# Two-block network on one core: the attentions with heads of 64 weigh standing values with scaled, turned weights, two heads beside each other

## The reference, cut to what matters

```python
p = softmax(concat([sink, s_loc, s_ctx]))[..., 1:]          # 8 heads
o = einsum(p[:span], v_near) + einsum(p[span:], v_ctx)      # 64 wide
o_x = concat([o, local_mixers(...)]) @ w_out
x = layer_norm(ALPHA * x + g1 * o_x, ln1_g, ln1_b)
```

```python
ya = sliding_window_attention(qa, ka, va, sinks) * silu(g_a)   # 2 key heads
yb = forgetting_attention(qb, kb, vb, log_f) * silu(g_b)       # 8 key heads
yc = rms_norm(ssd_chunked(...) * silu(z_c), ssm_norm_w)
x = x + concat([ya, yb, yc]) @ w_out
```

## Time and profile before

| | |
|---|---|
| median of 3 runs | 2305.1 us |
| the profiled execution | 2304.22 us, span 2302.4 us |
| TensorE busy | 2035.6 us, 88% of the span |
| VectorE, ScalarE, GpSimd busy | 786.6 us, 457.2 us, 189.7 us |
| mean granted TensorE clock | 0.985 |
| the chain that ended last | PE 62%, DMA 31%, DVE 4%, ACT 2% |
| weighing in attentions (L541) | 512 records, 65.5 us busy |
| turns (L507) | 332 records, 61.1 us busy |

### The profile page before, as it was taken

One profiled execution on the slowest core, in us unless ns is written; L12 is line 12 of the kernel. 1 busy time (PEld: TensorE's weight loads), 2 busy tenths in 40 slices (PEclk: granted clock), 3 DMA queues, 4 the chain that ended last, 5 costly groups with the idle time before them and its releaser, 6 DMA issues.

```text
span 2302.4 us, 30476 instructions
## 1 busy us (share of the span) xinstructions
PE 2035.6 (88%) x11971; PEld 1212.3 (53%) x11972; DVE 786.6 (34%) x1836; ACT 457.2 (20%) x1059; POOL 189.7 (8%) x240
## 2 busy tenths in 40 slices
PE   6999999799877789999877777798999999999998
PEld 4566566444433335757433333344875575775574
DVE  1355674111111116656111111114466312456413
ACT  2142112111111112411111111111123212123112
POOL 1000001111111110001111111111000000000000
PEclk9999999999999999999999999999999999999999
DMA  9235649999999985686999999996343332343230
GB/s 376 110 129 240 255 156 378 423 426 427 427 425 426 425 345 211 236 317 257 424 425 425 424 425 425 427 420 242 134 182 129 111 147 110 147 165 129 95 142 19
DMA packets 62872, 640.95 MB, mean 278 GB/s; under 512 B 15868, under 2 KB 16420, under 8 KB 24240
## 3 DMA queue, kind: packets, MB, share of 16 engines
q1 hardware_dynamic: 41728, 588.39, 61.9%
q0 software_dynamic: 19984, 44.74, 5.5%
q10 hardware_dynamic: 1056, 6.37, 0.7%
HBM read 622.50 MB, written 44.17 MB: 290 GB/s over the span
## 4 chain that ended last, share of the span: by engine, by line
PE 62%; DMA 31%; DVE 4%; ACT 2%; issue 1%; SPq 0%; POOL 0%; DVEq 0%
DMA ring<-in_moe 26%; PE ps L866 10%; PE ps L1037 10%; PE ps L519 8%; PE ps L1051 6%; PE ps L1148 5%; PE ps L507 3%; PE ps L695 3%; DMA ring<-in_denseA 3%; PE ps L1220 2%; PE ps L872 2%; PE ps L1016 2%; PE ps L541 2%; PE ps L771 2%; PE ps L584 1%; DMA ring<-in_denseB 1%
## 5 line engine op out<-in xcount | busy, mean ns | idle before, releaser
L866 PE MATMUL ps<-ring,scr 128*64 128x256 f32 (+1 forms) x4800 | 667.5, 430 | 178.2 <-DMA ring<-in_moe 169.3
L866 PEld LDWEIGHTS ps<-ring,scr 128*64 128x64 f32 x4800 | 333.4, 138 | 485.9 <-DMA ring<-in_moe 239.3
L1833 DVE TENSOR_TENSOR scr<-ps,scr 128x512 f32<-128x512 f32 (+3 forms) x98 | 54.6, 558 | 574.6 <-PE ps L866 487.0
L1037 PE MATMUL ps<-ring,hT 128*128 128x512 f32 (+1 forms) x576 | 245.5, 578 | 5.1 <-ACT hT L1546 5.1
L519 PE MATMUL ps<-ring,hT 128*128 128x512 f32 (+1 forms) x512 | 199.3, 547 | 0.5 <-ACT hT L1516 0.5
L1444 POOL DMA_INDIRECT ys_scratch<-scr,ytab x128 | 125.0, 976 | 825.4 <-DVE scr L2495 791.6
L1670 ACT ACTIVATE scr<-ps 128x512 f32<-128x512 f32 x64 | 38.2, 597 | 760.8 <-PE ps L866 694.0
L2495 DVE COPY scr<-ps 128x1024 f32<-128x1024 f32 x64 | 78.4, 1224 | 269.3 <-PE ps L866 243.4
L1037 PEld LDWEIGHTS ps<-ring,hT 128*128 128x128 f32 x576 | 108.1, 193 | 117.8 <-issue 108.2
L1516 ACT ACTIVATE scr<-ps 128x256 f32<-128x256 f32 (+2 forms) x168 | 71.3, 436 | 403.7 <-PE ps L507 403.7
L519 PEld LDWEIGHTS ps<-ring,hT 128*128 128x128 f32 x512 | 97.3, 193 | 93.0 <-issue 89.2
(11 more groups left out here) (330 smaller groups left out, 2019.2 us busy)
## 6 DMA issues: line engine op xcount, KB each, us to landing
ring<-in_moe SPq DMA_DIRECT2D x192, 2048.0 KB, 15.9
ring<-in_denseB SPq DMA_DIRECT2D x48, 2048.0 KB, 7.7
ring<-in_denseA SPq DMA_DIRECT2D x36, 2048.0 KB, 16.2
scr<-ys_scratch POOLq DMA_DIRECT2D x6, 1024.0 KB, 7.2
modB<-mod_scratch POOLq DMA_DIRECT2D x10, 512.0 KB, 11.3
ring<-kv_scratch SPq DMA_DIRECT2D x2, 2048.0 KB, 8.6
tok_scratch<-hb POOLq DMA_DIRECT2D x6, 512.0 KB, 2.9
memT_scratch<-modB ACTq DMA_DIRECT2D x2, 1024.0 KB, 6.7
```

The costliest lines, as they stand in the source:

```text
L866: last = mm(out, lhs(c)[:, 0:64], w(c)[:, half * q:half * (q + 1)], start=(c == 0), stop=(c == n - 1))
L1037: last = mm(T["open"][:, 0:cols], hT16[:, c, t * P:(t + 1) * P], w[:, c, 0:cols], start=(c == 0), stop=(c == DC - 1))
L1833: return V.tensor_tensor(out, a, b, op)
```

## The change

The function `attention` becomes two: `memory_attention` for the heads of 256, which keeps the old scheme, and `paired_attention` for the heads of 64. In this one

- VectorE takes the scores of two units, then waits for each unit's exponential, takes the reciprocal of its sum, and multiplies `sbuf_p` by it in place; a new semaphore `p_scaled` tells TensorE that it can turn. Then come the extras of two units. Pieces of the extras move by a unit or two;
- the sink's score is one more column in `sbuf_s`, so that the exponential's sum holds it; the question and answer about `esk` go;
- the values stand and the turned weights pass, 128 columns: the outputs come by columns, 64 by 128 queries for a head. An even head uses partitions 0 to 63 of the bank, an odd head 64 to 127; the products of two heads alternate by key block. A bank holds the 8 heads of 128 queries, and VectorE copies it;
- ScalarE takes both exponentials, then copies both turned units, then serves the questions of two units;
- the turns of the attentions' outputs go, in A (16 blocks in layer 0, 8 in layer 1) and in B (16 in each layer), with ScalarE's copies of them; the products with the output weights read `hb` and `mixB`. The norm's scratch rows move from `hb` to the place of `sbuf_pT`;
- the gates `ga` and `gb` of B come by columns, as the attentions' outputs now do.

The old functions are in the section above; the diff's core:

```diff
-TURNED = ("x0", "x1", "x2", "qb", "kb")
+TURNED = ("x0", "x1", "x2", "qb", "kb", "ga", "gb")
...
-    sbuf_s = cv(2, 512)
-    sbuf_p = cv(2, 512)
+    sbuf_s = cv(2, 516)
+    sbuf_p = cv(2, 516)
...
+        def turn_weights(i, nkc):
+            turn([sbuf_p[:, i % 2, k * P:(k + 1) * P] for k in range(nkc)])
+        def paired_attention(units, score, values, nkc, fill):
+            T["p"] += len(units)
+            for i in range(2):
                 score(*units[i])
+            fill(0)
+            for i in range(0, len(units), 2):
+                n, h = units[i]
+                for k in (i, i + 1):
+                    need("scaled", p_scaled)
+                    turn_weights(k, nkc(n))
+                    turned = T["tp"]
+                    if k == i:
+                        for at in range(i + 2, min(i + 4, len(units))):
+                            score(*units[at])
+                    if k > 0:
+                        fill(k)
+                if h == 0:
+                    T["bank"] = av_bank()
+                pe.wait_ge(tp_free, turned)
+                for b in range(nkc(n)):
+                    for q in range(2):
+                        last = mm(T["bank"][HD * q:HD * q + HD, h // 2 * P:(h // 2 + 1) * P], values(n, h + q, b),
+                                  sbuf_pT[:, q, b, :], start=(b == 0), stop=(b == nkc(n) - 1))
+                if h == NH - 2:
+                    last.then_inc(av_full, 1)
...
+        def memory_attention(units, score, values, beside):
...
-            for t in range(nt):
-                need("h", h_ready)
-                turn([hb[:, t, i * P:(i + 1) * P] for i in range(4)])
+            need("h", h_ready, nt)
...
-                    of_rows(mk_at - 2 + j, t, 0, 512)
+                    w = tile(mk_at - 2 + j)
+                    rows_times(lambda c: hb[:, t, c * P:(c + 1) * P] if c < 4 else hT8[:, c, t * P:(t + 1) * P],
+                               lambda c: w[:, c, :], 512)
...
-                if i == 12:
+                if i == 13:
                     pe.wait_ge(sums_ready, l + 1)
...
-                out_product(t, n, 0, lambda c: mixT[:, c, t * P:(t + 1) * P])
+                out_product(t, n, 0, lambda c: mixB[:, t, c * P:(c + 1) * P])
...
-            for t in range(NX):
-                need("h", h_ready)
-                for c in (0, 4):
-                    turn([mixB[:, t, (c + i) * P:(c + i + 1) * P] for i in range(4)])
+            need("h", h_ready)
+            out_attended(0, 0)
+            need("h", h_ready)
             pe.wait_ge(tp_free, T["tp"])
-            out_attended(0, 0)
             need("w", w_ready)
...
+        def weights(i, n, h, nk):
+            T["nm"] += 1
+            act.wait_ge(nm_ready, T["nm"])
+            A(sbuf_p[:, i % 2, 0:nk], sbuf_s[:, i % 2, 0:nk], ACT.Exp, bias=nm[:, n, h:h + 1],
+              accum_out=rsum[:, n, h:h + 1]).then_inc(p_ready, 1)
+        def paired_attention(units, nkc, sink, serve, after=None):
+            for i in range(0, len(units), 2):
+                for k in (i, i + 1):
+                    n, h = units[k]
+                    weights(k, n, h, P * nkc(n) + sink)
+                for k in (i, i + 1):
+                    copy_turned(sbuf_pT[:, k % 2, 0:nkc(units[k][0]), :], nkc(units[k][0]))
+                    if after:
+                        after(k)
+                if i > 0:
+                    serve(i - 1)
+                serve(i)
+            serve(len(units) - 1)
...
-                if i == (6 if l == 0 else 2):
+                if i == (6 if l == 0 else 3):
                     for_dve(lambda: A(rstd[:, 0:nt], rstd[:, 0:nt], ACT.Sqrt))
...
+        def paired_attention(units, keys, masks, cq, sink, finish, extra, ck=None):
+            def scores(i):
+                n, h = units[i]
+                bank = score_bank()
                 nk = keys(n)
                 s = sbuf_s[:, i % 2, 0:nk]
+                m = masks(n)
+                if sink:
+                    go(V.tensor_copy(sbuf_s[:, i % 2, nk:nk + 1], snk[:, h:h + 1]))
+                if m is None:
...
+                done()
+                least(n, h, s, sink)
+            def scaled(i):
+                n, h = units[i]
+                p = sbuf_p[:, i % 2, 0:keys(n)]
+                dve.wait_ge(p_ready, T["p"] + i + 1)
+                step(V.reciprocal(rinv[:, n, h:h + 1], rsum[:, n, h:h + 1]))
+                tell(ts(p, p, rinv[:, n, h:h + 1], None, ALU.mult), p_scaled)
+            for i in range(0, len(units), 2):
+                for k in (i, i + 1):
+                    scores(k)
+                for k in (i, i + 1):
+                    scaled(k)
+                if i > 0:
+                    extra(i - 1)
+                extra(i)
+                if i > 0 and units[i][1] == 0:
+                    finish(units[i][0] - 1, av_job())
+            extra(len(units) - 1)
+            finish(units[-1][0], av_job())
...
-                if i == 2:
+                if i == 3:
                     answer()
                     gate_moments((0, 1))
                     root()
-                if i == 4:
+                if i == 5:
...
+            def put_turned(n, bank):
+                tell(V.tensor_copy(hb[:, n, 0:512], bank), av_free)
                 tell(V.tensor_copy(mx[:, 1:2], mx[:, 0:1]), h_ready)
...
+                elif what[0] == "g":
+                    gate = (gaB if what == "ga" else gbB).rearrange("p t (c q) -> p c t q", c=4)
+                    read(tt(gate[:, 2 * part:2 * part + 2, :, :], bank.rearrange("p (c t q) -> p c t q", c=2, t=2),
+                            rB.rearrange("p (t q) -> p t q", t=2).unsqueeze(1).to_broadcast([P, 2, 2, P]), ALU.mult))
```

More of the change, by code:

```diff
@@ new lines, in memory_attention @@
+        def memory_attention(units, score, values, beside):
+            for i in range(2):
+                score(*units[i])
+            for i, (n, h) in enumerate(units):
+                need("p", p_ready)
+                turn_weights(i, 2)
+                turned = T["tp"]
+                if i + 2 < len(units):
+                    score(*units[i + 2])
+                beside(i)
+                pe.wait_ge(tp_free, turned)
+                if h % 2 == 0:
+                    T["bank"] = av_bank()
+                for k in range(2):
+                    last = mm(T["bank"][:, h % 2 * 256:(h % 2 + 1) * 256], sbuf_pT[:, i % 2, k, :], values(h, k),
+                              start=(k == 0), stop=(k == 1))
+                if h % 2 == 1:
+                    last.then_inc(av_full, 1)
@@ L1121, in fox_score @@
                    start=True, stop=True).then_inc(sc_full, 1)
[L1123 to L1124 removed]
+            paired_attention([(n, h) for n in range(NX) for h in range(NH)], fox_score,
+                             lambda n, h, k: vbB[:, k, h * HD:(h + 1) * HD], lambda n: n + 1, fill)
             stream(17)
@@ L1797, in _ @@
                 weighted_stream(t, 1, 2, l)
-            attention([(n, h) for n in range(NX) for h in range(4)], lambda n: 2, False, 4,
-                      after=lambda i: attended_turned(0) if i == 6 else None)
+            memory_attention([(n, h) for n in range(NX) for h in range(4)],
+                             lambda i: attended_turned(0) if i == 6 else None)
             attended_turned(1)
```

207 lines of the change are left out of this document (72 added, 135 removed).

## The result

After: 2318.06 us (median of 4 runs, 2316.12 to 2319.34). Before, in the same runs: 2303.98 us (4 runs, 2302.08 to 2305.42). Ratio 1.0058 [1.0045, 1.0071]: slower by 0.6%, where 2300 was forecast. The profiled execution took 2317.41 us (span 2315.6), against 2304.2 (span 2302.4) before.

What follows compares the result with a forecast made beforehand. TensorE carries most of the chain, DMA nearly all the rest; TensorE and VectorE are both at the limit in half of B's second attention. -3.2 + 3.5 - 4.4 = -4.1 us from 2304.2: forecast 2300, own range 2294 to 2306, overall 2286 to 2310.

Steps and rivals of the forecast that it cites:

- A layer 0: Block A's first attention: tile released 2.0 us earlier, stage -3.2 us (bounds -2 and -5).
- the column of sums is turned one head later: Block B, each layer: the sums' last load, landing 2 us before VectorE wants it, comes later; 0.7 us lost.
- the GELU's wait: A layer 0: GELU on ScalarE now precedes the next exponential, so TensorE waits; loss 2.2 us.
- A layer 1: Block A's second attention: heavy VectorE pairs delay the tile and the row's write; +3.5 us (bounds +2.5 and +5).
- Weighing: Attention's weights times values, values standing: 0.054 us a record and 0.14 a group; 19.2 us gained if all on the path.
- The three pairs of B: Second attention of block B: TensorE waits for VectorE in three pairs, 0.8, 0.9 and 1.2 us a layer.
- The tails: Behind block B's second attention: the turning of 16 blocks goes, 3.2 us gained a layer.
- The signs that the prediction named for being right: Weighing records 0.05 to 0.06 us apart, TensorE waiting for scaling, no gap after the 1777 product, later A layer 1 row write.
- those for being wrong: No waits of TensorE for scaling, or 0.108 us a weighing record, or an A layer 1 no longer than before.
- The second: Rival: array halves do not run beside each other in weighing, 0.108 us a record; 13.4 over forecast, 2313 us; chance 0.12.
- The third: Rival: block B's tail gives nothing, the output product waits for gated rows; 6.4 back, 2306 us; chance 0.10.
- The first: Rival: VectorE's work stays covered in the attentions, block B gaining 6.4 a layer; -21, 2283 us; chance 0.21.

Runs made afterwards that it cites:

- e1: Changed kernel with block B's column of sums taken, turned and copied earlier, so its load is issued sooner; 2305.02 us, ratio 1.000.
- e2: Changed kernel with the convolution passes beside block B's second attention spread out where pairs are heavy; 2309.82 us, ratio 1.0024.
- e5: Changed kernel with block A's norm loads issued ahead of GpSimd's wait for the last modulation row; 2315.2 us, ratio 1.0038.
- e4: Changed kernel plus 16 unused matmul records a layer filling the wait at the start of B's second attention; 2313.23 us, ratio 1.004.
- best2: Changed kernel with column of sums early, convolutions spread and A layer 1's two 1024-column passes moved; 2297.75 us, ratio 0.9961.
- e3: Changed kernel with A layer 1's two passes of 1024 columns moved from extras 3 and 5 to 2 and 9; 2311.53 us, ratio 1.0028.

## Why the prediction was wrong, step by step

The miss in the span is 17.3 us: A layer 0 5.9, block B 6.5 a layer, less 1.5 of luck in the first loads.

**The step that failed most** is, in block B, "the column of sums is turned one head later, some 2 us, ... 0.7 lost", with 0.6 for the start. In layer 0 of the kernel after, the column's turn came 3.25 us later against the attention's start, the load 2.1 us longer, and it landed some 5.5 later, against a margin of 2.8 on VectorE (it wanted the load at 1698.66 before; the prediction took 2). From the first scores to the second half product it took 10.52 us (1699.90 to 1710.42) for 6.88 before (1696.25 to 1703.13), and that product took 1.67 longer by the clock: 5.3 us where 1.3 stood. So the delay was too short by half, the longer transfer and the clock were priced at nothing. e1 took 5.1 to 5.6 back.

**A term that was missing**: the clock behind long waits. Waits were priced as their own length. At the start of block B's second attention the traces of all kernels hold 15 waits of 2.06 to 5.31 us, each with a fall of the clock, and 7 of 0.42 to 1.41 without one. From the turn behind the wait to the next weighing it takes 4.39 or 4.40 us in the seven, and 5.97 to 7.38 in the fifteen, 1.6 to 3.0 more. Behind the GELU's wait of 2.37 the turn and the scores paid 1.4; behind the waits of 1.1 to 1.5 in A layer 1's attention nothing was paid. The length alone does not decide: e1 waits 3.65 us for a tile in A layer 1 and keeps its clock, where the kernel after waits 3.61 (982.42) and has 0.72 over 982 to 988; and behind a wait of 1.54 (1060.85) it has 0.72 over 1060 to 1066. TensorE of e1, and its busy times by stretch:

```profile
985.87 1.96 PE L595 MATMUL ps<-ring,small 128*32 128x128 f32 x64 [3.65 <-DMA ring<-in_denseA]
```

```profile
980.00:1003.00 23.00, 15.92 (x338) 13.07 (x332) 15.06 (x43) 5.91 (x13) 0.61 (x1) 1.00 1.01 427
```

At 274 a wait of 0.86, with others ahead of it, went with a clock of 0.72 where before had 0.86: from the first router product to the second it took 20.76 us for 19.10.

**Weighing** had the right price, 0.054 a record and 0.14 a group, but not all of its neighbours: a product ahead of a group of the new form takes 3.54 us instead of 3.46, and the turn behind it 0.05 longer, some 0.13 a group. The trace of before could not show that. For the 8 groups of an attention of block B that is 1.0: the first attentions gained 0.8 where 1.6 stood, and in the second it takes most of the 1.3. With the pairs' waits removed (e2) a pair gained 0.07 against the 8.98 of the earlier trace rows. The Trainium skill, page "TensorEngine Tiling (Array Packing)", section "Tiling Modes" (Key Properties), says that a change of the mode drains TensorE; that these 0.13 us are this drain fits it, but no run here took the change of mode away.

**A layer 0.** Three steps failed here, all counted from the attention's start. The tile was to be released 2.0 earlier and came 1.0 later (85.16 us for 84.15). The GELU's wait was right (2.37 for 2.2); the first turn waited 1.14 for 0.5, and two more waits took 0.97 (0.66 and 0.31) for 1.4. The clock behind the GELU, 1.4, and the eight groups at 0.13, 1.0, were not in the sum. Together that is most of the 3 us. The turning of 16 blocks at the end was to give 2 by going: in its place TensorE waits 2.99 us (241.60) for VectorE's last extras and the copy of the outputs, and the products with the output weights start 0.85 us earlier (134.64 for 135.49) and not 4. The norm's load was to land 2 earlier and landed 2.3 later (152.79 for 150.48), so that the turn behind the products waits for the norm (0.86 at 273.95), which it did not before. The row ahead of the load was written later (issued after 115.35 us for 111.95), but by e5 an issue 12 us earlier hardly moves that landing; what sets it is open. In the six executions with this code in A layer 0 (after, e1 to e4, best2) the stage took 810.39 to 813.25, +0.4 to +3.3 against the one execution before, so a part of the +2.68 is chance; the -3.2 is outside in each.

**Right**: A layer 1, +3.31 for +3.5, by the mechanism named (waits of 1.11, 1.49, 1.36 and 1.30 us; the write at 995.07, before 988.01; e3 took 3.0 back). The three pairs of B, 2.82 (layer 1: 3.19) for 2.9. The tails, -3.14 for -3.2. The signs that the prediction named for being right came, save that the kernel was not ahead in A layer 1, and none of those for being wrong: they watched the terms that had a price, and the load that failed was not among them.

**The rivals.** The second, 0.108 a record, is refuted: the result was slower, near its 2313, but not by it. The third is refuted: the output product starts 17.63 us after the product behind the last weighing (1778.84 to 1796.47), without a wait. The first, that VectorE's cover holds, did not happen in this kernel; in best2, with the extras rearranged, block B gives 4.3 a layer of its 6.4.

## What to carry to other kernels

When a change adds work to an engine that runs beside the bound one, every result that its queue sends on a round trip through memory is to be followed to its use: the issue's delay, the longer transfer and the margin at the landing. A long wait is to be priced with the clock that may fall behind it, here 1.4 to 3.0 us more. Here what cost most was repaired by moving side work to places with slack, not by making the added work shorter: e1, e2 and e3 move lines only, and turn +0.6% into -0.4%. A turn that is taken out gives its time only if nothing else is awaited there: 3.1 us in block B's tail, next to nothing in A layer 0.

## What the runs showed of the hardware

Two heads in the two halves of the array run beside each other if their records alternate (16 in 1.02 us, 0.054 a record and 0.14 a group), in part if 8 of one half follow 8 of the other (1.51), and about as well in runs of 4 (8 in 0.60) and of 2 (4 in 0.37). A small write that GpSimd issued at 225.57 was awaited by its program until 253.78, with the DMA engines busy throughout (share 1.01 over 226 to 254), and loads that were issued 12 us earlier landed 1.3 us sooner, no more than executions differ by (151.98 to 153.51 us from the attention's start where nothing was changed).
